# Routing tables, early cache pages and constants in a hybrid decoder layer: one change in three stages

## What is computed

```
hn = rms_norm(x, norm_mix_w)
q, k, v, f_logit, u = split(hn @ w_in)             # w_in is 1024 x 2056: 3*512, 8 heads, 512
attn = forgetting attention of q over the cache pages (samples) or over the prompt
ssm  = S5 scan of u, then a gated linear unit
x = x + concat(rms_norm(attn), rms_norm(ssm)) @ w_out
h = rms_norm(x, norm_ffn_w)
score = sigmoid(h @ w_router)                      # 64 experts
idx = top_k(score + router_bias, 8); g = 2.5 * score[idx] / sum(score[idx])
acc[token] += g * (silu(h @ w_gate_e[e]) * (h @ w_up_e[e])) @ w_down_e[e]    # for its 8 experts
y = x + acc + shared expert
```

## Time and profile before

| | |
|---|---|
| median of 3 runs | 1470.42 us (1466.45 to 1475.05) |
| the profiled execution, its own time | 1469.02 us |
| its span in the trace | 1467.3 us |
| TensorE's granted clock, mean of the span | 0.964 of full |
| PE busy | 1348.2 us, 92% |
| DVE / ACT / POOL busy | 619.4 / 346.1 / 246.0 us |
| moved by DMA | 424.20 MB, mean 289 GB/s |

### The profile page before, as it was taken

How to read it: one execution, slowest core, us unless ns; L and a number is a source line. 1 busy time by engine, 2 the same in 40 slices (tenths; PEclk the granted TensorE clock), 3 DMA queues, 4 the chain that set the end, 5 groups by cost and what they waited for, 6 DMA issues and landing times. The chain is left out here.

```text
span 1467.3 us, 29978 instructions
## 1 busy us (share of the span) xinstructions
PE 1348.2 (92%) x9894; PEld 718.7 (49%) x9895; DVE 619.4 (42%) x1853; ACT 346.1 (24%) x939; POOL 246.0 (17%) x291
## 2 busy tenths in 40 slices
PE   6999899999999999889988889999999999899991
PEld 3445566566667786534643234444444443333330
DVE  1524156676666665343762222323323332233234
ACT  1203235344433443330101011111111111111110
POOL 2000110005083320000000111222122221122120
PEclk9999889999999999999898999999999999999996
DMA  7412299999999999971038999999999999999976
GB/s 318 74 29 51 87 316 292 332 369 310 339 305 309 339 322 330 362 271 65 22 134 337 383 376 370 354 351 375 343 373 356 359 345 358 372 362 364 360 242 209
DMA packets 160689, 424.20 MB, mean 289 GB/s; under 512 B 48225, under 2 KB 51842, under 8 KB 134402
## 3 DMA queue, kind: packets, MB, share of 16 engines
q1 hardware_dynamic: 142928, 381.30, 71.1%
q0 software_dynamic: 14400, 38.82, 10.6%
q10 hardware_dynamic: 3250, 2.65, 0.6%
HBM read 395.25 MB, written 41.06 MB: 297 GB/s over the span
## 5 line engine op out<-in xcount | busy, mean ns | idle before, releaser
L2634 PE MATMUL ps_gu<-ring,mixT 128*32 128x512 f32 (+3 forms) x1664 | 352.4, 617 | 22.2 <-SPq L2452 21.3
L2634 PEld LDWEIGHTS ps_gu<-ring,mixT 128*32 128x32 f32 (+2 forms) x1664 | 120.6, 137 | 249.8 <-issue 232.5
L2653 PE MATMUL ps_y<-w_dn,aT_e 128*32 128x512 f32 (+3 forms) x832 | 175.9, 598 | 3.2 <-DVE aT_e L2567 0.6
L1509 PE MATMUL ps_kT<-ident,ring 128*128 128x128 f32 x1024 | 141.9, 281 | 14.3 <-DVE ring L1132 5.4
L1509 PEld LDWEIGHTS ps_kT<-ident,ring 128*128 128x128 f32 x1024 | 114.3, 144 | 72.8 <-ACT ring L967 34.3
L1791 POOL DMA_INDIRECT kT<-h_dram,idx x50 | 51.9, 1037 | 453.5 <-DVE idx L1825 453.5
L1132 DVE COPY ring<-ps_kT 128x512 f32<-128x512 f32 x128 | 88.2, 689 | 85.2 <-PE ps_kT L1509 82.8
L2565 DVE TENSOR_TENSOR act_in<-sil,ps_gu 128x256 f32<-128x256 f32 x48 | 20.2, 421 | 244.2 <-ACT sil L2510 244.2
L2510 ACT ACTIVATE sil<-ps_gu 128x256 f32<-128x256 f32 x48 | 18.4, 383 | 356.3 <-PE ps_gu L2634 356.3
L2476 POOL DMA_INDIRECT sums_dram<-qT,sidx x48 | 76.4, 1592 | 150.3 <-DVE qT L2575 143.2
L2653 PEld LDWEIGHTS ps_y<-w_dn,aT_e 128*32 128x32 f32 (+2 forms) x832 | 55.4, 132 | 93.4 <-issue 83.2
(11 more groups left out here) (566 smaller groups left out, 1690.5 us busy)
## 6 DMA issues: line engine op xcount, KB each, us to landing
ring<-in_cache_k SPq DMA_DIRECT2D x256, 256.0 KB
ring<-in_cache_v SPq DMA_DIRECT2D x256, 256.0 KB, 4.8
ring<-in_w_gate_e SPq DMA_DIRECT2D x64, 1024.0 KB
ring<-in_w_up_e SPq DMA_DIRECT2D x64, 1024.0 KB
w_dn<-in_w_down_e SPq DMA_DIRECT2D x64, 1024.0 KB
w_in<-in_w_in SPq DMA_DIRECT2D x8, 1028.0 KB, 18.5
sums_dram<-w_dn SPq DMA_DIRECT2D x1, 4608.0 KB, 21.5
ring<-in_w_out SPq DMA_DIRECT2D x2, 2048.0 KB, 12.9
```

The source lines that it names most:

```text
L1509: last = pe.transpose(ps_kT[:, j % 2, e * PAGE:(e + 1) * PAGE], k_places[n % RING][:, e * DA + j * P:e * DA + (j + 1) * P], m.ident[:, :])
L2634: last = pe.matmul(ps_gu[at, :].rearrange("p (g n) -> p g n", g=2), xgT[:, u, k, at], w_gu[:, place, :, k, :].rearrange("p s g n -> p (s g ...
L2653: last = pe.matmul(ps_y[at, n, :], aT[:, j, at], w_dn[:, place, j, n * 512:(n + 1) * 512].rearrange("p s n -> p (s n)"), start=(j == 0), s ...
```

## The change

The edits, in the order of the stages:

1. **Constants.** The block of its own is gone. `fill_constants` is the first thing on POOL in `project`, the identity and the ones first. ACT waits for `ident_made` ahead of its first activation, DVE and PE wait for `constants_made` ahead of their first work.
2. **Projection's weights.** The ring of `mixers` is allocated in `project`. The q, k and v columns of `w_in` (1536 of 2056) are loaded into the ring's K and V places, slice by slice; the 8 forget columns come by one transfer of 32-byte runs into `w_f`, behind x tile 2; the `u` columns come by one transfer into the space of the transposed keys, behind all x tiles.
3. **Early pages.** At the end of `project`'s stores of k, v and bias rows, SP waits for `v_mm` of the last tile and loads K groups 0, 1, 2 and V groups 0, 1. The stores of logf and `u_scr` come behind them. `u_scr` has a semaphore of its own, for which SP waits in `mixers` ahead of the third V group, and no longer at the end of `project`.
4. **First turn.** The K transposes of turn 0 stand in the prologue: parts 0 and 1 ahead of the transpose behind the exponentials, parts 2 and 3 behind it. DVE's copies of parts 1 and 3 move with them.
5. **Ranks in bf16.** `mask` is bf16, and ACT makes bf16 copies of the triangle and of the ones. The ranks take one bf16 matmul each.
6. **Gate parts.** ACT writes the three bf16 parts into `pick`. DVE makes the two subtractions behind `entry`, and column 3 of `pick` right behind them, all ahead of its wait for `exp_mm`. 5 of the 8 slices of the shared matmul `shared(1, 0)` stand ahead of `entries`.
7. **Registers.** Each engine reads the loop numbers behind its first steps in `experts`.

```diff
+def fill_constants(pool, m, ident_made, constants_made):
+    pool.memset(m.ident[:, :], 0.0)
+    pool.memset(m.ones[:, :], 1.0)
+    pool.drain()
+    pool.affine_select(out=m.ident[:, :], in_=m.ident[:, :], compare_op=ALU.not_equal, fill=1.0, base=0,
+                       pattern=[[-1, P]], channel_multiplier=1)
+    pool.drain()
+    pool.sem_inc(ident_made, 1)
...
+    pool.sem_inc(constants_made, 1)
...
+    m.ring = sb("ring", [P, 2 * RING * PLACE + KT], F32)
...
-                    sp.dma_start(w_in[:, k, :], a["w_in"][0, k * P:(k + 1) * P, :]).then_inc(w_loaded[k], 16)
+                    sp.dma_start(w_q(k), a["w_in"][0, k * P:(k + 1) * P, 0:3 * DA]).then_inc(w_loaded[k], 16)
...
+                x_rows(2)
+                columns_of = a["w_in"][0].rearrange("(k p) n -> p k n", p=P)
+                with nc.allow_non_contiguous_dma(reason="runs of 32 bytes"):
+                    sp.dma_start(w_f[:, :, :], columns_of[:, :, 3 * DA:3 * DA + NH]).then_inc(w_f_loaded, 16)
+                for t in range(3, TT):
                     x_rows(t)
+                sp.dma_start(w_u, columns_of[:, :, 3 * DA + NH:D_IN]).then_inc(w_u_loaded, 16)
...
+                sp.wait_ge(v_mm, TT)
+                sp.wait_ge(table_in, 32)
+                for n in range(RING):
+                    load_pages(nc, sp, m, a["cache_k"], m.k_places[n], m.k_in[n], n)
+                    if n < RING - 1:
+                        load_pages(nc, sp, m, a["cache_v"], m.v_places[n], m.v_in[n], n)
                 sp.wait_ge(logf_done, 1)
...
-                    sp.dma_start(m.u_scr[c * P:(c + 1) * P, :], m.uT[:, c, :]).then_inc(stored, 16)
+                    sp.dma_start(m.u_scr[c * P:(c + 1) * P, :], m.uT[:, c, :]).then_inc(m.u_stored, 16)
...
-                key_pages(0)
-                bias_rows(0)
-                key_pages(1)
-                value_pages(0)
-                key_pages(2)
-                bias_rows(1)
-                value_pages(1)
-                bias_rows(2)
-                value_pages(2)
+                for q in range(3):
+                    bias_rows(q)
+                sp.wait_ge(m.u_stored, 16 * KS)
+                value_pages(RING - 1)
...
                 last.then_inc(new_mm, 1)
+                pe.wait_ge(c_12_sb, 2)
+                pe.wait_ge(k_in[0], 16 * GRP)
+                k_transposes(0, 0)
+                k_transposes(0, 1)
                 pe.wait_ge(exp_new, 1)
                 pe.transpose(ps_t[0:T_S, 0:ROWS], ...).then_inc(pTn_mm, 1)
+                k_transposes(0, 2)
+                k_transposes(0, 3)
                 pe.wait_ge(pTn_sb, 1)
...
-        mask = sb("mask", [P, TT, NE], F32)
+        mask = sb("mask", [P, TT, NE], BF16)
+        tri_bf, ones_bf = sb("tri_bf", [P, P], BF16), sb("ones_bf", [P, P], BF16)
...
+                act.wait_ge(gates_done, 1)
+                act.copy(m.pick[:, :, :, 4], gate[:, :, :]).then_inc(high_done, 1)
                 shared_silu(0)
+                act.wait_ge(resid_done, 1)
+                act.copy(m.pick[:, :, :, 5], resid[:, :, :]).then_inc(mid_done, 1)
+                act.wait_ge(part_done, 1)
+                act.copy(m.pick[:, :, :, 6], part[:, :, :]).then_inc(low_done, 1)
...
-                dve.tensor_copy(m.pick[:, :, :, 4], gate[:, :, :])
...
+                dve.wait_ge(high_done, 1)
+                tt(resid[:, :, :], gate[:, :, :], m.pick[:, :, :, 4], ALU.subtract).then_inc(resid_done, 1)
+                dve.tensor_copy(cnt_i[:, 0, :], order)
...
+                dve.wait_ge(mid_done, 1)
+                dve.drain()
+                tt(part[:, :, :], resid[:, :, :], m.pick[:, :, :, 5], ALU.subtract).then_inc(part_done, 1)
+                tt(m.pick[:, :, :, 3], ..., ALU.subtract).then_inc(pick_done, 1)
                 dve.wait_ge(exp_mm, 1)
...
-                            last = pe.matmul(ps[:, 3, t * NE:(t + 1) * NE], (m.tri_strict if s == t else m.ones)[0:rows(s), :], mask[0:rows(s), s, :],
+                            last = pe.matmul(ps[:, 3, t * NE:(t + 1) * NE], (tri_bf if s == t else ones_bf)[0:rows(s), :], mask[0:rows(s), s, :],
...
+                shared(1, 0, range(0, 5), 0)
                 entries()
-                shared(1, 0, range(KD), 0)
+                shared(1, 0, range(5, KD), 0)
...
-                n_two, n_mixed, n_four, n_loops = registers(nc, ENG.PE, m.loop_tab, 0, 4, 3, MAX_LOOPS)
...
                     step_of(step, 16 * (step // 2 + step % 2 + 1), step % 2, needed, TWO[step % 2], piece)
+                n_two, n_mixed, n_four, n_loops = registers(nc, ENG.PE, m.loop_tab, 0, 4, 3, MAX_LOOPS)
```

More of the change, by code:

```diff
@@ new lines, in load_pages @@
+def load_pages(nc, sp, m, cache, place, arrived, n):
+    ids = nc.values_load_multi_w_load_instructions(m.page_row[0:1, n * GRP:(n + 1) * GRP], engines=(ENG.SP,), min_val=0, max_val=N_POOL - 1,
+                                                 skip_runtime_bounds_check_because="a page table holds numbers of pages of the pool")[1]
+    for i in range(GRP):
+        sp.dma_start(place[:, i * DA:(i + 1) * DA], cache[0, bass.ds(ids[i], 1)].rearrange("n k h d -> (n k) (h d)")).then_inc(arrived, 16)
@@ L329, in _ @@
             def _(pool):
+                fill_constants(pool, m, ident_made, constants_made)
                 pool.memset(seq_after[:, :], 1.0)
@@ L479, in _ @@
             def _(pe):
+                pe.wait_ge(constants_made, 1)
                 pe.wait_ge(vec_loaded, 16 * 6)
@@ L525, in _ @@
                             for i, out in enumerate((pq[0:n, 0, :], pq[0:n, 1, :], pv[0:n, :])):
-                                last = pe.matmul(out, tok(k), w_in[:, k, i * DA:(i + 1) * DA], start=(k == 0), stop=(k == KD - 1))
+                                last = pe.matmul(out, tok(k), w_q(k)[:, i * DA:(i + 1) * DA], start=(k == 0), stop=(k == KD - 1))
                                 if k == KD - 1 and i:
@@ L754, in mixers @@
         skip_done, z_done, glu_s, glu_mm, gate_done = (sem(x) for x in ("skip_done", "z_done", "glu_s", "glu_mm", "gate_done"))
-        def pages(sp, cache, place, arrived, n):
-            ids = nc.values_load_multi_w_load_instructions(m.page_row[0:1, n * GRP:(n + 1) * GRP], engines=(ENG.SP,), min_val=0, max_val=N_POOL - 1,
-                                                         skip_runtime_bounds_check_because="a page table holds numbers of pages of the pool")[1]
-            for i in range(GRP):
-                sp.dma_start(place[:, i * DA:(i + 1) * DA], cache[0, bass.ds(ids[i], 1)].rearrange("n k h d -> (n k) (h d)")).then_inc(arrived, 16)
         def y_out(engine, k):
@@ L2527, in _ @@
                 dve.sem_inc(y_dve, 1)
-                n_loops = loops(ENG.DVE)
                 def destinations(u, step, turn):
```

123 lines of the change are left out of this document (63 added, 60 removed).

## The result

The changed kernel took 1458.0 us, the median of 12 runs (1450.1 to 1464.1); the kernel before 1469.5 (12 runs, 1463.6 to 1475.7). The ratio is 0.9913, with a 95% interval of 0.989 to 0.9937, so 12.8 us less, between 9 and 16. The difference is under 1%, but the interval stays clear of 1. The forecast was 1458.3.

A forecast was written before the change was run, and what follows sets the result against it. It took PE to set the pace in `mixers`, with DMA close behind, and weight landings to start PE's stretches in `experts`. Terms 2.9 + 1.3 + 1.5 + 2.8 + 4.4 - 0.8 = 12.1 us off the 1470.4 median gave 1458.3; range 1451 to 1466.

The forecast's parts named there:

- Start, 2.9: Start of `project`: without a separate constants block SP issues its first transfer at about 1.0, saving 2.9 us (2.4 to 3.1).
- First token tile, 1.3: First tile in `project`: smaller weight slices shorten PE's waits, saving 1.3 us more (0 to 1.6).
- The wait of 0.83 at 28.62 goes too: First token tile: PE's 0.83 us wait vanishes, as slices take PE 2.6 us and arrive every 2.0.
- Stage end, 1.5: End of `project`: SP's 1.7 us wait for the fourth `u_scr` store leaves the path, saving 1.5 us (0 to 1.7).
- First turn, 2.8: Start of `mixers`: turn 0's K transposes move into PE's wait for the exponentials, saving 2.8 us (0.5 to 4.5).
- Net 4.5 - 0.9 - 0.8: Mixers' turn 0: its 4.5 us, less 0.9 for prompt scores that stay and 0.8 for later parts, gives 2.8 us.
- Ranks, 4.4: Router's ranks: 20 bf16 matmuls replace 40 float32 records, so DVE starts 4.4 us earlier (2.1 to 4.9).
- Tables, 0.8 of loss: Routing tables: 3.5 us of DVE work put into its 2.77 us wait delays them 0.8 us (0.3 to 1.5).
- Experts, costed at nothing: `experts`: PE's first step gains some 5 us and register reads move, but next steps await weight landings; nothing counted.
- The first (the mixers give it back): DMA, not PE, bounds `mixers`, so the 8.5 us gained before is lost at its end: 1466.8; chance 0.07.
- The second: `experts`: PE's lead moves gathers and scatters into the DMA hole at 792, about 4 us more: 1454.3; chance 0.18.
- The third (`w_f` is the wait): `project`: PE waits for the forget columns' load of 1024 short runs; 1491 at 0.04 us each; chance 0.03.

The follow-up runs named there:

- `w_f` late: The changed kernel with the forget columns' load issued last of all weights, behind x tiles 3 and 4 and the u columns; ratio 0.9946 to the kernel before.
- turn 0 in the loop: The changed kernel with the transposes and copies of K group 0 back in the mixers' loop, pages still early; ratio 0.9941 to the kernel before.
- The front alone: The kernel before with the change only up to the end of the mixers, routing as before; ratio 0.9956, 6.5 us less.
- fifth early: The changed kernel with the fifth expert's gate and up weights issued before SP waits for the fourth slot's landing; ratio 0.9863 to the kernel before.
- entries first: The changed kernel with the entries' matmuls ahead of the first five slices of the shared matmul; ratio 0.9904 to the kernel before.
- the route alone: The kernel before with the change only from the router on; ratio 0.9951, 7.2 us less.
- column late: The changed kernel with DVE's second subtraction and column 3 of `pick` behind the tables; ratio 0.99 to the kernel before.
- the fifth early in the kernel before: The kernel before with only the fifth expert's weights issued ahead of the wait for the fourth slot; ratio 0.9982.
- registers first: The changed kernel with PE's, DVE's, ScalarE's and GpSimd's loop registers read ahead of the first expert steps; ratio 0.9922 to the kernel before.

## Why the prediction was right in sum, and where not

The sum of 12.1 met 12.8, but three terms and one zero were off.

**Start, 2.9: right.** 3.1 at SP. **First token tile, 1.3: too small.** The first slice gained 0.3 beyond SP's 3.1, as forecast. From there to the forget columns it took 23.2 us, before 25.1, so 1.9 and not the 0.83 of the earlier trace rows. The two terms are 5.3 instead of 4.2. The step that failed is "The wait of 0.83 at 28.62 goes too", which took the rest of the pass as fixed: that wait went, and the first slice took 4.15 us (11.42 to 15.57) where it had taken 5.05 (14.82 to 19.87). PE's weight loads began 0.86 us apart at first and 0.43 apart later, as at the two levels of the clock, and the pace changed 3.0 us behind PE's start here and 4.9 before (the granted clock reads 1.00 throughout, so the column does not show this change). This part is chance: with the same new front the pace changed between 3 and 6 us behind the start, and nine profiles have PE at the forget columns at 34.6 to 35.8, in the mean 35.2. The three with the old front have 39.9, 40.3 and 40.4. So the two terms are 5.0 in the mean, and 4.2 lies inside the spread. `w_f` landed inside its forecast of 30 to 32, with the 2.9 us of cover that are left when PE comes at 34.6 and not at 35.7. The Trainium skill, DMA: Bandwidth & Descriptors, section Specifications, would have it slow below 512 bytes, and the page gives each contiguous run a descriptor of its own (its rule on a non-contiguous last dimension is for single elements, where `w_f` has runs of 8). The trace agrees with both, with about one small packet per run and a lower rate while they passed, but the price was 0.6 us and no wait (`w_f` late).

**Stage end, 1.5: right,** 1.6.

**First turn, 2.8: too large.** Turn 1's transposes did come 3.1 earlier against the kernel with turn 0 in the loop, but 1.7 were left at turn 2. "Net 4.5 - 0.9 - 0.8" priced the gap at the lower clock and forgot that a gap won inside a slow stretch is filled with work that is slow too: in these two traces the clock rose at 195.4 and 195.8, and did not come earlier by the 3.1 us that PE's work did. Against the kernel before, whose clock rose at 193.7, turn 2 stands only 1.2 nearer to the stage's start (23.9 and 22.7).

These four give 5.3 + 1.6 + 1.7 = 8.6, beside the forecast's 8.5. The front alone measured 6.5, interval 2.8 to 10.3. In the changed kernel's profile no more than 2.4 of it is seen at the end of the mixers: `mix_and_route` began at 633.32, before at 635.75. Up to the last copy that is the clock.

Executions with the same pattern of lower clock can be set side by side. With one short fall in `project` (3.4 us) the last copy ended at 170.80 in the kernel before, at 166.72 (fifth early) and 166.65 (entries first) with the new front. With three falls, 10 us in all, it ended at 175.36 (the route alone) and at 169.87 (column late). With three falls, 17 us in all, it ended at 177.97 (the fifth early in the kernel before) and between 171.46 and 172.96 in six kernels with the new front. That is 4.1, 5.5 and 5.0 to 6.5 less, like with like, and old and new fronts occur in all three patterns. So the falls do not need the change, and over all runs the mean clocks are alike (0.9626 in 76 runs of the kernel before, 0.9635 in 12 of the changed one).

`mixers` itself then takes 454.0 to 460.6 us with the new front and 456.0 to 461.5 with the old, a spread that hides the 1.7. In the mean `mix_and_route` began at 629.8 in the eight kernels with the whole new front and all loads in their place, and at 636.3 in the three with the old one: 6.5 earlier, as the front alone measured.

**Ranks, 4.4: too small by 0.4 in these two traces, and 3.5 to 3.8 by the two others with the old route.** "I take one record per matmul at the price of a float32 one" failed: the trace has 0.05 us for one (1.05 / 20), not 0.115. The trace has 4.8 in all, and the gates end last. By the rule of the Trainium skill, TensorE: Matmul & The Clock Gate, section on weight-path perf modes, the term was 4.9. The trace agrees with the rule itself: a weight load took 0.098 us in bf16 and 0.192 in float32 at the upper clock.

**Tables, 0.8 of loss: about right.** From the entries to `load_tab` it is 4.8 us now, before 3.8 (750.56, in the trace of before, to 754.37). ScalarE's second copy takes 1.44 us, and DVE waited 0.93 for it, so "ACT's second copy hides beside the small ones" was wrong. VectorE had made the same copy in 0.79:

```profile
725.46 0.79 DVE L2102 CAST pick<-gate 128x320 bf16<-128x320 f32 x1
```

Together the first weights are 3.7 nearer to the scores; 3.6 was forecast.

**Experts, costed at nothing: wrong, by about 3 us.** "The next steps wait for landings, so I cost it and the moved register reads at nothing" held for the register reads (registers first: same time). It failed for the rest. From the first weights to the end of the span it took 710.1 us in the kernel before and 710.8 with the front alone, and 704.5 to 709.5, in the mean 707.5, in the nine kernels with the new route and the old order of SP. From the first gate load to the seventeenth it is 152.1 us in the kernel before and 153.7 with the front alone, and 146.7 to 150.5 in those nine (the expectations, which count from nought, call it the sixteenth). The hole is the same. What differs is the rate at which full queues deliver. Windows from 40 to 75 us behind the first weights, in the kernel before, with the front alone, in the changed kernel, and in the one with the entries first:

```profile
797.24:832.24 35.00, 30.37 (x155) 11.31 (x153) 8.95 (x31) 3.22 (x9) 4.27 (x3) 0.90 1.00 371
```

```profile
792.61:827.61 35.00, 30.97 (x160) 11.75 (x160) 10.22 (x32) 3.61 (x13) 4.92 (x4) 0.95 0.99 367
```

```profile
792.97:827.97 35.00, 26.72 (x142) 10.06 (x138) 7.31 (x24) 3.22 (x9) 2.79 (x3) 0.85 1.00 387
```

```profile
787.10:822.10 35.00, 28.13 (x154) 10.69 (x152) 8.96 (x28) 3.22 (x9) 3.69 (x4) 0.90 1.01 387
```

The share is 1.00 in each, but 371 and 367 GB/s stand against 387 and 387. The same window gives 384 to 389 in all nine kernels, and 372 for the fifth early in the kernel before. At 4% over 35 us that is 1.5 us, and the rest comes in the stretch behind it. Neither the register reads nor the slices nor the fourth slot's issue alone takes it away. What all nine share, and no run took back, is that PE's first gate matmul stands 19.6 to 21.4 us behind the first weights and not 23.0 to 23.3, and the first scatter goes out at 37.1 to 39.2 and not at 40.9 to 41.8. The cause is not settled.

**The rivals.** The first (the mixers give it back) fell with the front alone. The second had the right outcome in the experts, some 3 more, and its mechanism is there in part: the third gather went out 31.6 to 33.7 us behind the first weights in the nine kernels and 35.4 to 36.3 with the old route. By the packets of the indexed queue, its 0.37 MB passed between 32 and 36 in the changed kernel, ahead of the fifth load; in the kernel before more than half of it, and with the front alone nearly all, passed behind 38, beside that load. But 0.37 MB are no more than 1 us at 380 GB/s (an estimate), so that alone is not the 3. That the time came out at the forecast and not at this rival's 1454.3 is the front, which came in under its terms. The third (`w_f` is the wait) is far off: it takes 2.75 MB more ahead of the load to make PE wait 5 us.

So 12.8 is 6.5 from the front and 7.2 from the route, less 0.9 that their intervals cover. A right sum of partly wrong terms, which is luck as far as the sum goes.

## What to carry to other kernels

A chain of landings is moved by whatever lets the first of them start, and by every hole in it: here the queues stood empty for 4 us because SP waited for four landings and then read eight numbers before it issued the next load, and moving one wait behind one issue was worth 3.8 us (standard error 1.6) in the changed kernel and 2.8 (0.9) in the kernel before. Matmuls whose operands are zeros and ones belong in bf16, where both are exact, but look first at what else the waiting engine does in their shadow: by the trace of before the gate parts held DVE until 729.45, so the ranks without them could give 0.9 us and not 4.8 (no run has one without the other). Compare single executions only where their patterns of granted clock agree.

## What had not been expected of the hardware

- Executions of the same kernel differ by 14 us (1450.1 to 1464.1) with a mean granted clock of 0.969 to 0.957; over 199 runs 0.001 of clock goes with 1.1 us. In `project` the same matmuls ran with 3.4, 10 or 17 us at the lower level, with the old front and the new.
- A rank in bf16 (128x128 weights, 64 columns) took 0.05 us, in float32 0.23 at the upper clock and 0.46 at the lower for its two records.
- ScalarE takes 1.44 us to copy 128x320 values as bf16 into every seventh place of `pick`; DVE took 0.79 for the same copy, and 1.41 for column 3, a subtraction of two values that it writes there.
- Queues at a share of 1.00 moved 367 to 389 GB/s, by kernel and not by chance, it seems: 371, 367 and 372 with the old route, 384 to 389 in nine kernels with the new.
